# A fused two-block kernel on one core: key products placed inside the attention steps, gate row placed behind the experts

## What is computed

```python
mod = jax.nn.silu(c) @ w_mod + b_mod
shift, scale, gate = jnp.split(mod[:, None, :], 3, axis=-1)
h = rms_norm_2(x, g_pre) * (1 + scale) + shift
q, k, v, g_att, u, g_lru, merge = split(h @ w_in)
# three groups of four heads of 128, with dilation 1, 4 and 16
y_a = (dilated_attention(q, k, v) * jax.nn.silu(g_att)) @ w_pa
...
out = (gate_a * y_a + gate_b * y_b) @ w_o
return x + gate * rms_norm_2(out, g_post)
```

## Time and profile before

| what | value |
|---|---|
| runs | 3099.05, 3095.88, 3095.96 us; median 3095.96 |
| profiled execution | 3096.4 us |
| its span on the engines | 3094.3 us, so 2.1 us lie around it |
| PE busy | 2939.5 us (95%) |
| DVE, ACT, POOL busy | 1722.3, 1275.9, 545.3 us |
| chain that ended last | PE 35% of the span, ACT 3%, DVE 2% |

### The profile page before, as it was taken

One profiled execution on the slowest core, in us unless ns is written; L12 is line 12 of the kernel. 1 busy time (PEld: TensorE's weight loads), 2 busy tenths in 40 slices (PEclk: granted clock), 3 DMA queues, 4 the chain that ended last, 5 costly groups with the idle time before them and its releaser, 6 DMA issues. The chain is left out here.

```text
span 3094.3 us, 35406 instructions
## 1 busy us (share of the span) xinstructions
PE 2939.5 (95%) x13630; PEld 2399.8 (78%) x13630; DVE 1722.3 (56%) x1791; ACT 1275.9 (41%) x1409; POOL 545.3 (18%) x285
## 2 busy tenths in 40 slices
PE   7998999988999999999999979989799899999999
PEld 7586777846888888888888867878788678677887
DVE  6577112497888888888888873120200332786132
ACT  2013001325777777777777753130301310334021
POOL 0002323100001110000001012303122033333330
PEclk9998999999999999999999999999999799999999
DMA  3011102269999999999999942101111311111131
GB/s 117 14 37 48 41 34 71 107 263 382 372 380 380 372 382 383 382 384 370 379 380 377 380 191 89 51 32 55 45 45 45 100 69 66 37 41 48 48 123 55
DMA packets 122739, 555.07 MB, mean 179 GB/s; under 512 B 17840, under 2 KB 17872, under 8 KB 89456
## 3 DMA queue, kind: packets, MB, share of 16 engines
q1 hardware_dynamic: 112096, 523.51, 44.1%
q0 software_dynamic: 5488, 20.61, 2.4%
q10 hardware_dynamic: 5056, 9.54, 0.8%
HBM read 521.41 MB, written 31.03 MB: 179 GB/s over the span
## 5 line engine op out<-in xcount | busy, mean ns | idle before, releaser
L2225 DVE TENSOR_TENSOR slots_lo<-buffer,slots_hi 128x2048 fp32r<-128x2048 f32 x384 | 852.8, 2286 | 152.4 <-ACT slots_hi L1571 152.4
L1571 ACT ACTIVATE slots_hi<-buffer 128x2048 fp32r<-128x2048 f32 x384 | 710.2, 1921 | 51.8 <-PE bank L1178 27.0
L911 PE MATMUL bank<-hT_hi,ring_hi 128*128 128x512 f32 x1216 | 482.8, 397 | 16.2 <-issue 13.3
L912 PE MATMUL bank<-hT_lo,ring_hi 128*128 128x512 f32 x1216 | 475.7, 391 | 0.0
L913 PE MATMUL bank<-hT_hi,ring_lo 128*128 128x512 f32 x1216 | 475.5, 391 | 0.0
L812 POOL TENSOR_TENSOR ring_lo<-buffer,ring_hi 128x1024 fp32r<-128x1024 f32 x115 | 292.4, 2545 | 54.6 <-ACT ring_hi L1411 46.1
L809 POOL CAST ring_hi<-buffer 128x1024 fp32r<-128x1024 f32 x105 | 117.3, 1117 | 987.7 <-DMA buffer<-in_wstream 978.3
L911 PEld LDWEIGHTS bank<-hT_hi,ring_hi 128*128 128x128 f32 x1216 | 230.1, 189 | 69.7 <-issue 16.9
L912 PEld LDWEIGHTS bank<-hT_lo,ring_hi 128*128 128x128 f32 x1216 | 230.1, 189 | 49.6 <-issue 2.6
L913 PEld LDWEIGHTS bank<-hT_hi,ring_lo 128*128 128x128 f32 x1216 | 229.8, 189 | 48.3
L1178 PE MATMUL bank<-slots_hi,xsT_hi 128*128 128x512 f32 x960 | 257.6, 390 | 2.4 <-DVE buffer L2240 2.4
(11 more groups left out here) (438 smaller groups left out, 4235.2 us busy)
## 6 DMA issues: line engine op xcount, KB each, us to landing
buffer<-in_w_gate SPq DMA_DIRECT2D x128, 1024.0 KB, 6.3
buffer<-in_w_up SPq DMA_DIRECT2D x128, 1024.0 KB, 5.0
buffer<-in_w_down SPq DMA_DIRECT2D x128, 1024.0 KB, 8.2
buffer<-in_wstream SPq DMA_DIRECT2D x154, 512.0 KB, 3.6
buffer<-in_x SPq DMA_DIRECT2D x16, 512.0 KB, 7.3
od<-buffer ACTq DMA_DIRECT2D x24, 260.0 KB, 2.0
xacc<-buffer SPq DMA_DIRECT2D x8, 512.0 KB, 2.6
h2d<-buffer SPq DMA_DIRECT2D x8, 512.0 KB, 4.8
```

Source lines behind the costliest of these rows:

```text
L911: mm(bank, lhs[0], rhs[0], start=first, stop=False)
L912: mm(bank, lhs[0], rhs[1], start=False, stop=False)
L1571: fn(slots_hi[:, n_ % NH, :], slots[n_ % NS], ACT.Copy).then_inc(slot_high_ready, 1)
L2225: tt2(slots_lo[:, place_of(n_), :], slots[n_ % NS], slots_hi[:, n_ % NH, :].bitcast(F32), ALU.subtract).then_inc(slot_split, 1)
```

## The change

It does six things:

1. In groups 1 and 2 the key products are made in the attention steps of the group before (`side_fill`): step tt of group g makes key tile tt of group g + 1, its first half (four of the eight pieces) behind the scores, its second behind the transposes of the probabilities. The steps of group 2 make four of the eight gate tiles (f = 0 and 1), each over two steps, in quarters.
2. DVE instead of ACT drains these (`side_there`), one step later, behind the maxima of the step. Keys get a second buffer; the gate tiles are stored raw, and ACT applies silu to both features at once behind the attention.
3. The weight stream has keys ahead of queries in groups 1 and 2, and `last_fill_of_tile` follows.
4. `GATT_ORDER` behind the attention has only the gate tiles of f = 2 and 3 left; two stand ahead of the first turn, and the last two turns stand together.
5. The gate row is made behind the last expert's first rows and ahead of the turned activations, from a buffer of its own (`gate_ring`) that SP loads when slots 21 and 23 of the last expert have been used. The copy of `scB`, the load of `rowrep` and the two DVE operations on GATE move behind the experts.
6. SP loads slots 8 to 11 of the first expert only once the first gather has landed, and no longer waits for the gate row's tiles; POOL no longer waits for the stores of h2 ahead of the gather.

The diff, cut to this:

```diff
...
@@ -109,10 +111,10 @@
     if i < I_ATT:
-        return 0, ("gaterow", (i - I_GATEROW) // 4)
+        return 1, ("gaterow", (i - I_GATEROW) // 4)
...
         g, o = divmod(i - I_ATT, 12)
-        return 1, ("Q", g, 2 * o + 1) if o < 4 else (("K", g, 2 * (o - 4) + 1) if o < 8 else ("V", g, 7))
+        return 1, ("KQ"[o // 4 == (g > 0)], g, 2 * (o % 4) + 1) if o < 8 else ("V", g, 7)
...
     if i < I_LRU:
@@ -134,11 +136,12 @@
-GATT_ORDER = [("gatt", f, 0) for f in range(4)]
+GATT_ORDER = [("gatt", 2, 0), ("gatt", 2, 1)]
+for _i in range(2):
+    GATT_ORDER += [("OT", _i, 0), ("gatt", 3, _i)]
 for _i in range(4):
-    GATT_ORDER += [("OT", _i, 0), ("gatt", _i, 1)]
-for _i in range(4):
-    GATT_ORDER += [("OT", 4 + _i, 0), ("GA", _i // 2, _i % 2)]
+    GATT_ORDER += [("OT", 2 + _i, 0), ("GA", _i // 2, _i % 2)]
+GATT_ORDER += [("OT", 6, 0), ("OT", 7, 0)]
...
     LRU_TILES += [("lu", 2 * _q + _c) for _c in range(2) if _q < 4]
@@ -220,30 +223,37 @@
     for j in range(2):
-        b.add(("gaterow", j), "act")
-    for j in range(2):
...
+def side_fill(g, tt):
+
+    if g < 2:
+        return ("K", g + 1, tt), 0, 1
+    return ("gatt", tt // 4, tt // 2 % 2), tt % 2, 2
...
         b.add(("last", j // 2, j % 2), "dve")
+    for j in range(2):
+        b.add(("gaterow", j), "act")
...
     for g in range(3):
-        for j in (0, 2, 4, 6):
+        for j in (0, 2, 4, 6) if g == 0 else ():
             b.add(("Q", g, j), "dve")
-            for i in range(8, 16 if g == 0 and j == 0 else 8):
+            for i in range(8, 16 if j == 0 else 8):
...
             b.add(("hT", j), "act" if j % 2 else "dve")
-        for j in (1, 3, 5, 7):
+        for j in (1, 3, 5, 7) if g == 0 else range(8):
             b.add(("Q", g, j), "dve")
-        for j in range(8):
+        for j in range(8 if g == 0 else 0):
...
             b.add(("V", g, tt), "dve" if tt % 2 else "act")
@@ -259,6 +269,9 @@
                 b.add(("PT", g, tt, w), "act")
+            key, part, parts = side_fill(g, tt)
+            if part == parts - 1:
+                b.add(key, "dve")
...
         b.add((kind, x) if kind == "OT" else (kind, x, y), "dve" if kind == "OT" else "act")
@@ -455,8 +468,9 @@
         chosen = at(38 * K + 256, CAP)
-        rowrep = at(24 * K, 2, DM)
-        scB = at(22 * K, KD, P)
+        rowrep = at(48 * K, 2, DM)
+        scB = at(13 * K, KD, P)
+        gate_ring = at(16 * K, 8, KD, P)
...
         gateT = at(50 * K + 24, NE)
...
@@ -496,8 +510,8 @@
         dn_ = at(43 * K + 416, NT, HEADS)
-        Oin = [at(o, 3, GW) for o in (44 * K, 45 * K + 512, 36 * K, 38 * K)]
-        sga = at(32 * K, HEADS, SEQ)
+        Oin = [at(32 * K + 3 * GW * i, 3, GW) for i in range(4)]
+        sga = at(44 * K, HEADS, SEQ)
...
         mt2 = at(48 * K, 4, HALF)
...
@@ -724,15 +740,13 @@
             load_slot(0, 1)
-            for i in range(I_GATEROW, I_ATT):
-                load_tile(i)
...
                 load_slot(0, n)
-            for j in range(2):
-                b1.wait_drained(sp, ("topT", j))
+            b1.wait_drained(sp, ("topT", 1))
+            sp.wait_ge(xs_loaded, 16)
...
             with sp.Fori(0, NE - 1) as e:
@@ -757,6 +771,11 @@
                 load_tile(i)
+            for h in range(2):
+                sp.wait_ge(slot_used, (NE - 1) * 24 + 22 + 2 * h)
+                for i in range(4 * h, 4 * h + 4):
+                    sp.dma_start(gate_ring[:, i].rearrange("p k n -> p (k n)"),
+                                 a["wstream"][I_GATEROW + i]).then_inc(gate_loaded[h], 16)
...
                 sp.dma_start(xfd[tt * P:(tt + 1) * P, :], xf3[:, tt, :]).then_inc(xf_stored, 16)
@@ -845,8 +864,6 @@
                                     ALU.mult).then_inc(gain_ready, 1)
-            pool.wait_ge(h2_stored, 16 * NT)
-            pool.dma_start(rowrep.rearrange("p a b -> p (a b)"), a["rowrep"]).then_inc(rows_loaded, 16)
...
             def gather():
@@ -872,13 +889,13 @@
             pool.wait_ge(xs_loaded, 16 * NE)
-            pool.wait_ge(mod_ready, 1)
...
             b2.wait_full(pool, ("hT", 15))
+            pool.dma_start(rowrep.rearrange("p a b -> p (a b)"), a["rowrep"]).then_inc(rows_loaded, 16)
...
                 step(nc.gpsimd.memset(m, 0.0))
@@ -912,16 +929,17 @@
-            def split_feature_tile(b, key, w, rhsT, h, nk, split=None):
-
-                bank = b.wait_free(pe, key)
+            def split_feature_tile(b, key, w, rhsT, h, nk, split=None, first=0, end=None):
+
+                bank = b.bank(key) if first else b.wait_free(pe, key)
                 hs = slice(h * HALF, (h + 1) * HALF)
-                for k in range(nk):
+                for k in range(first, end or nk):
...
                                         k == 0, k == nk - 1)
-                return last.then_inc(b.full, 1)
+                if end is None or end == nk:
+                    last.then_inc(b.full, 1)
...
                 for j in range(first, end):
...
@@ -1233,23 +1239,31 @@
             last_rows(0, 4)
+            pe.wait_ge(scB_ready, 1)
+            for h in range(2):
+                bank = b2.wait_free(pe, ("gaterow", h))
+                pe.wait_ge(gate_loaded[h], 64)
+                for k in range(KD):
+                    last = mm(bank[:], scB[:, k, :], gate_ring[:, 4 * h:4 * h + 4, k, :], start=(k == 0), stop=(k == KD - 1))
+                last.then_inc(full2, 1)
...
                 per = 8 // ORDER[g]
-                for i, j in enumerate((0, 2, 4, 6, 1, 3, 5, 7)):
+                first_k, first_q = (base + 4, base) if g == 0 else (base, base + 4)
+                for i, j in enumerate((0, 2, 4, 6, 1, 3, 5, 7) if g == 0 else range(8)):
...
                         transposed_activations(b2, "hT", xin3, xn_ready, 16, 8, 16)
-                    w = wait_split_tile(pe, base + f)
+                    w = wait_split_tile(pe, first_q + f)
...
                         last_rows(4, 8)
-                for f in range(4):
-                    w = wait_split_tile(pe, base + 4 + f)
+                for f in range(4 if g == 0 else 0):
+                    w = wait_split_tile(pe, first_k + f)
...
@@ -1282,6 +1296,11 @@
                         scores(tt + 1)
+                    key, part, parts = side_fill(g, tt)
+                    f, h_ = (key[2] // 2, key[2] % 2) if g < 2 else key[1:]
+                    w_side = wait_split_tile(pe, (I_ATT + 12 * (g + 1) if g < 2 else I_GATT) + f)
+                    k0, dk = KD // parts * part, KD // parts // 2
+                    split_feature_tile(b2, key, w_side, hT_parts, h_, KD, None, k0, k0 + dk)
...
                     for w_ in range(nw):
@@ -1289,6 +1308,7 @@
                         last.then_inc(full2, 1)
+                    split_feature_tile(b2, key, w_side, hT_parts, h_, KD, None, k0 + dk, k0 + 2 * dk)
...
                     for h in range(HEADS):
...
@@ -1588,8 +1601,6 @@
             slots_high(0, 1, 2, first_ones=True)
-            gate_row(0)
-            gate_row(1)
...
             slots_high(0, 4, 5, first_ones=True)
@@ -1624,6 +1635,8 @@
                     nc.scalar.activation(root[:, 0:1], ident[:, 0:1], ACT.Sqrt)
+                    act.wait_ge(slot_used, e * 24 + 19)
+                    nc.scalar.copy(scB, silu_c.unsqueeze(2).to_broadcast([P, KD, P])).then_inc(scB_ready, 1)
...
                         fn(last_hi[:, h * HALF:(h + 1) * HALF], psum[6 + h][:], ACT.Identity,
@@ -1652,6 +1665,9 @@
                 fn(q_[:, :, 4 * h:4 * h + 4], q_[:, :, 4 * h:4 * h + 4], ACT.Sqrt).then_inc(f_root, 1)
+                for c in range(2 - 2 * h):
+                    bank = b2.wait_full(act, ("gaterow", c))
+                    fn(GATE[:, c * HALF:(c + 1) * HALF], bank[:], ACT.Copy).then_inc(drained2["act"], 1)
...
                     hs = slice(h * HALF, (h + 1) * HALF)
@@ -1666,11 +1682,10 @@
                 r = ORDER[g]
-                for j in range(8):
+                for j in range(8 if g == 0 else 0):
...
                     bank = b2.wait_full(act, ("K", g, j))
-                    dst = Kh[:, f, :].rearrange("p (r l) -> p r l", r=r)[:, :, h * HALF // r:(h + 1) * HALF // r]
-                    fn(dst, bank[:].rearrange("p (l r) -> p r l", r=r), ACT.Copy).then_inc(drained2["act"], 1)
+                    fn(Kh[g][:, f, h * HALF:(h + 1) * HALF], bank[:], ACT.Copy).then_inc(drained2["act"], 1)
...
                 else:
@@ -1714,6 +1729,9 @@
+            for f in range(2):
+                b2.wait_drained(act, ("gatt", f, 1))
+                fn(sga[:, f, :], sga[:, f, :], ACT.Silu).then_inc(gatt_ready, 1)
...
                     act.wait_ge(d_ready, 1)
@@ -2240,11 +2258,7 @@
-            b1.wait_drained(dve, ("gaterow", 1))
-            dve.wait_ge(rows_loaded, 16)
-            step(stt(scale, scale, 1.0, cols[:, COLS["pre"][0]:COLS["pre"][0] + 8], ALU.add, ALU.mult))
-            step(tt2(GATE, GATE, rowrep[:, 0, :], ALU.add))
-            tt2(GATE, GATE, rowrep[:, 1, :], ALU.mult).then_inc(mod_ready, 1)
```

(31 more changed lines are left out.)

26 lines of the change are left out of this document (8 added, 18 removed).

## The result

The changed kernel took 3025.36 us (median; 3023.87 to 3026.42) beside 3097.51 for the kernel before (3095.88 to 3100.94): ratio 0.9765, 95% interval 0.9748 to 0.9782. The forecast was 3020 (3009 to 3036). The profiled execution took 3026.18, its span is 3024.4 us (before 3094.3) at a clock of 0.986 (0.977). PE is busy for 2912.3 us instead of 2939.5: the number of matmuls is the same, and so is busy time times clock (some 2872 us at full clock in both), so these 27 us are the same work done at a higher clock. The other 43 us of the 70 are time in which PE waited.

What follows compares the result with a forecast made beforehand. PE was taken as the bound, so only its waits and low clock could give time back. Gains 9.8 - 0.3 + 22.6 + 27.9 + 2.0 + 2.9 + 11.5 = 76.4 us, from 3096.4, gave 3020 us (3009 to 3036).

Steps and rivals of the forecast that it cites:

- part C: Attention: key or gate tiles inside the steps fill PE's waits; gains 22.6, 27.9 and 2.9 us in groups 0, 1, 2.
- part A: Ahead of the first expert: gate row taken out, so indices turn earlier and the gather lands sooner; gain 9.8 us (6.4 to 10.5).
- part D: Behind group 2: fewer gate tiles remain, PE waits about 7.2 us before the first turn; gain 11.5 us (6 to 15).
- its own 0.74 us: Attention step: PE idles 0.74 us after the transposes until ACT has copied them; half a tile (2.72 us) covers it.
- The clock terms: First tiles behind groups 0 and 1 no longer run slow, since busy steps keep the clock; gain 1.0 us each (0 to 1.7).
- Part B: Behind the last expert: gate row products fill PE's 13.45 us idle time before the transposes; cost 0.3 us (0 to 3).
- the second chain: Ahead of the first expert: modulation columns (4.4 us if cold), then DVE's remainders and a copy, end at 711.7 us too.
- Rival R2: Attention steps: POOL's splits block DVE through the shared port; half to all of 29 us, middle 22, giving 3042; chance 0.07.
- R1: Attention: the halves lengthen ACT's round instead of filling it, PE's 55 us of waits remain, giving 3075 us; chance 0.05.
- R3: Group 2: clock stays low at 0.67 as PE still waits; 61.5 us instead of 48, giving 3033; chance 0.07.
- R4: Behind the last expert: gate row is not hidden, 10 to 14 us return, giving 3032 us; chance 0.04.
- R5: Attention steps: side tiles' weights come late, ten tiles cost 102 us without prefetch, giving 3122, slower; chance 0.02.

Runs made afterwards that it cites:

- whole_tile_ahead: Changed kernel with the whole side tile (in group 2 the whole half) between scores and transposes of the probabilities, nothing behind the transposes: 3038.74 us, ratio 0.9805.
- exp_earlier: Changed kernel with ACT's exponential of the combination weights one place earlier, behind the drain of the first gate tile instead of the second: 3020.78 us, ratio 0.9744.
- its two siblings: Changed kernel with a third gate tile ahead of the first turn: 3023.80 us; changed kernel with POOL's later weight splits held until the last turn: 3021.83 us.
- the edits together: Changed kernel with exponential earlier, later splits held, modulation columns first, DVE held until the gather is made, and another gate tile order: 3008.02 us, ratio 0.9700.
- columns_first: Changed kernel with the modulation columns' products, and DVE's addition on them, ahead of the turn of the indices: 3021.49 us, ratio 0.9750.

## Why the prediction was right, and where it was not

The mechanism was right where most of the gain was to come from. That the total is off by only 5 us is partly luck, since errors of both signs cancel: the three groups of part C gave 5.1 us more than forecast, part A 1.9 less, part D with the cold products behind it 5.5 less, and 3.6 us more passed upstream of the change's front and in the experts, mostly by chance.

**Part C held, step by step, and it has most of the gain.** PE's waits in groups 0 and 1 are gone (0.4 us left in each). The steps cost 9.92 us where I had summed 10.3: my terms were lengths of records, which overlap, and the distance of two starts is shorter; hence 25.0 and 29.7 us gained for 22.6 and 27.9. That the second half covers its own 0.74 us is shown by `whole_tile_ahead`. In group 2 the wait is 0.45 us in most steps, not 0.6. The clock terms came as forecast (0.8 and 1.0).

**Part B held in its cost, but not in what was to show it.** The net cost is 0.9 us here, within its bounds. But the transposes start 19.04 us behind the last rows instead of 17.36, so they moved by 1.7 us where the text allowed 1: the last rows themselves ran at the low clock here (5.31 us to the gate row, as in four other kernels; 3.75 in the remaining six that have it there). The transposes give it back, 3.66 us instead of 6.25. From the last rows to group 0 the changed kernels need 165.6 to 169.6 us, the two profiled with the old place 166.1 and 166.2, so 0.3 and 0.9 can't be told apart.

**Part A failed in one term.** The gather took 4.4 us: under the 5.5 I took, above the 3.6 of a weight tile and above the 3.2 of the fit that the prediction quotes. So the second chain decided, as the text allowed. I had put the modulation columns at 4.4 us, "slower if cold": they took 6.96, 2.6 more, and the first product came 13.55 us behind the turn of the indices where my sum had 11.1. With the columns out of the way it was 11.96, and with the gather undisturbed too, 10.04. Of the 9.8 us forecast 7.9 came in the front. The +1.4 in the experts' line was not in the sum: the first expert products start at the low clock, and the sixth row of them (four products each) stands 7.51 us behind the first instead of 6.08. In the other kernels with the gate row moved these rows take 6.3 to 7.4 us, so most of this comes and goes between executions and is no term of the change. With the 2.2 us of chance upstream, this leaves 4.4 us at the last rows. The forecast was also made against an execution whose gate row happened to find its weights early; against the kernel's median the part gives 7 to 10.

**Part D was mis-sized, by a term given to the wrong place.** The wait before the first turn (7.0 for 7.2) and that ahead of the projection (5.2 for 5.4) were right. The whole was not: 66.4 us instead of 62.2, and 1.4 more behind it, where the first products of the projection run at the low clock (10 us at 0.72; 1.00 before). The sum follows PE, and on PE three terms were short: the last two turns (1.2 us) are not in it, the cold clock took about 3 us instead of 2, and PE waited 0.86 and 2.41 us more for DVE between the turns where I had 1.

The path was wrong too, for DVE's chain is what ended last. It reads: 18.1 us to the first turn, 8.8 for that turn and the gate tile behind it (at a clock of 0.65; a tile and a turn took 5.95 before), 0.9 for ScalarE's silu, 38.5 of DVE without a gap, 0.1 to the projection: 66.4. Of the 38.5, 10.0 are excess beside POOL's splits. I had priced these collisions inside the attention steps, found slack there, and added nothing. Inside the steps they do happen at no cost: the maximum operation took up to 2.12 us, and PE waited 0.4 in the whole stretch. They cost where no slack is. The kernel before lost 8.8 us of DVE's time behind group 2 as well, but there DVE had gaps of 12.9 us; the changed kernel lost 12.8 and had one gap.

My reading of `exp_earlier` and its two siblings was too simple as well. "DVE bounds the stretch" let me expect 3.9 to 8 us of each, and each gave 0.9 to 2.6, because the chain is passed between engines: a gate tile that DVE waits for (3.90 us in the changed kernel, 5.43 in `exp_earlier`), POOL's splits beside it, and ScalarE's high parts behind PE's turns. Only the edits together gave 11.7, down to 54.7 us with 48.3 of PE's own work. How much each of them has in that was not taken apart.

Rival R2's mechanism thus was there, in another place than its own and at less than its price of 22 us; R1, R3 (clock 1.00 in group 2), R4 and R5 (no wait for side tiles) did not occur. The Trainium skill ("SBUF — State Buffer", who interferes with whom) says that a VectorE instruction with two SBUF inputs and a GpSimd instruction that reads SBUF contend for the shared ports, and that the later one waits for the whole of the earlier. The excess times agree: the addition of 2.74 us ends 0.55 us behind the split, the multiplication of 3.93 us 1.62 us behind its own. The same section reports that such two-input operations did not stall a DMA; the gather here differs, and the measurement decides: in `columns_first` its instruction ended at 705.82, 0.92 us behind the end of DVE's first subtraction, which had begun 0.17 us ahead of it. I weighed this rule only for the steps; it should have been carried to every stretch in which DVE is busy nine tenths of the time.

(The sums of groups 0 and 1 come out at 80.6 and 73.1 us from their terms, 0.1 and 0.2 from the figures given; nothing hangs on it.)

## What to carry to other kernels

Work that needs nothing from a ring of two engines fills the ring's waits one by one: put a piece of it into each wait, and size it by that wait. When a wait of the bound engine is removed, look which engine has the least idle time in the next stretch, and what runs beside it on the port that it shares. A short operation behind idle time can have the price of the low clock; put it right behind earlier work, ahead of the idle time.
